# Down-projection weight units taken in pairs, six matmuls in a row to one PSUM bank

## What is computed

```python
def swiglu(h, w_gate, w_up, w_down):
    return (jax.nn.silu(h @ w_gate) * (h @ w_up)) @ w_down

h = rms_norm(x, g_ffn1_pre[l])
x = x + 0.5 * rms_norm(swiglu(h, w_ffn1_gate[l], w_ffn1_up[l], w_ffn1_down[l]), g_ffn1_post[l])
```

## Time and profile before

| | |
|---|---|
| median of 3 runs | 1585.07 us (1584.85 to 1587.95) |
| span of the profiled execution (its whole time isn't recorded apart from the runs above) | 1583.4 us |
| TensorE matmuls busy | 1535.9 us (97%), 6549 |
| VectorE busy | 638.3 us (40%) |
| ScalarE busy | 495.1 us (31%) |
| GpSimd busy | 96.5 us (6%) |
| mean granted TensorE clock | 0.985 of 2.4 GHz |

### The profile page before, as it was taken

One profiled execution on the slowest core, in us unless ns is written; L12 is line 12 of the kernel. 1 busy time (PEld: TensorE's weight loads), 2 busy tenths in 40 slices (PEclk: granted clock), 3 DMA queues, 4 the chain that ended last, 5 costly groups with the idle time before them and its releaser, 6 DMA issues.

```text
span 1583.4 us, 17821 instructions
## 1 busy us (share of the span) xinstructions
PE 1535.9 (97%) x6549; PEld 1213.2 (77%) x6549; DVE 638.3 (40%) x753; ACT 495.1 (31%) x689; POOL 96.5 (6%) x145
## 2 busy tenths in 40 slices
PE   6999999999999979999999999899999999999996
PEld 5888888888888767666657887678888888888884
DVE  4433333333333473435545444463333333333334
ACT  4312212222222343445554232332212222222222
POOL 1000000000000040321220000220000000000001
PEclk9999999999999979999999999899999999999997
DMA  6333333333222212111112334133333333322211
GB/s 208 94 106 93 93 106 93 93 102 107 95 93 93 79 53 82 53 53 54 34 34 68 99 86 133 54 93 93 93 101 93 98 94 93 117 94 93 93 40 54
DMA packets 201007, 138.67 MB, mean 88 GB/s; under 512 B 4448, under 2 KB 188816, under 8 KB 200848
## 3 DMA queue, kind: packets, MB, share of 16 engines
q1 hardware_dynamic: 200160, 135.28, 28.7%
q10 hardware_dynamic: 816, 2.98, 0.5%
HBM read 136.14 MB, written 2.10 MB: 87 GB/s over the span
## 4 chain that ended last, share of the span: by engine, by line
PE 93%; DVE 5%; ACT 1%; DMA 1%; issue 0%; ACTq 0%; POOL 0%; DVEq 0%
PE ps L378 28%; PE ps L379 28%; PE ps L380 28%; PE ps L578 2%; DVE h_lo L916 1%; PE ps L555 1%; DVE ys L911 1%; PE ps L503 1%; PE ps L505 1%; PE ps L504 1%; PE ps L542 1%; PE ps L559 1%; PE ps L546 1%; DVE acc L943 1%; DVE w_lo L888 1%; DMA x_tok<-x 1%
## 5 line engine op out<-in xcount | busy, mean ns | idle before, releaser
L378 PE MATMUL ps<-h_hi,w_hi 128*128 128x512 f32 x1312 | 525.0, 400 | 9.7 <-DVE h_lo L916 7.3
L380 PE MATMUL ps<-h_hi,w_lo 128*128 128x512 f32 x1312 | 512.5, 391 | 0.0
L379 PE MATMUL ps<-h_lo,w_hi 128*128 128x512 f32 x1312 | 512.5, 391 | 0.0
L888 DVE TENSOR_TENSOR w_lo<-w_raw,w_hi 128x1024 fp32r<-128x1024 f32 (+1 forms) x260 | 311.4, 1200 | 172.3 <-ACT w_hi L655 164.1
L378 PEld LDWEIGHTS ps<-h_hi,w_hi 128*128 128x128 f32 x1312 | 247.3, 188 | 79.9 <-issue 24.7
L379 PEld LDWEIGHTS ps<-h_lo,w_hi 128*128 128x128 f32 x1312 | 247.4, 189 | 53.0 <-issue 3.4
L380 PEld LDWEIGHTS ps<-h_hi,w_lo 128*128 128x128 f32 x1312 | 247.2, 188 | 52.5
L655 ACT ACTIVATE w_hi<-w_raw 128x1024 fp32r<-128x1024 f32 (+1 forms) x260 | 257.6, 1019 | 32.5 <-PE ps L380 25.2
L380 PE MATMUL ps<-a_hi,w_lo 128*128 128x512 f32 x512 | 202.2, 395 | 0.0
L378 PE MATMUL ps<-a_hi,w_hi 128*128 128x512 f32 x512 | 202.2, 395 | 0.0
L379 PE MATMUL ps<-a_lo,w_hi 128*128 128x512 f32 x512 | 202.2, 395 | 0.0
(11 more groups left out here) (140 smaller groups left out, 998.4 us busy)
## 6 DMA issues: line engine op xcount, KB each, us to landing
w_raw<-w_ffn_gate SPq DMA_DIRECT2D x64, 512.0 KB, 4.0
w_raw<-w_ffn_up SPq DMA_DIRECT2D x64, 512.0 KB, 4.0
w_raw<-w_ffn_down SPq DMA_DIRECT2D x64, 512.0 KB, 3.3
w_raw<-w_in SPq DMA_DIRECT2D x44, 512.0 KB, 3.8
w_raw<-w_out SPq DMA_DIRECT2D x8, 512.0 KB, 3.7
w_raw<-w_proj_sb SPq DMA_DIRECT2D x8, 256.0 KB, 2.6
w_raw<-w_proj_ret SPq DMA_DIRECT2D x8, 256.0 KB, 2.5
out<-x_tok SPq DMA_DIRECT2D x8, 256.0 KB, 2.7
```

The costliest lines, as they stand in the source:

```text
L378: pe.matmul(ps[:, bank, :], wh, src_hi, start=first, stop=False)
L379: pe.matmul(ps[:, bank, :], wh, src_lo, start=False, stop=False)
L380: return pe.matmul(ps[:, bank, :], wl, src_hi, start=False, stop=last)
L888: dve.tensor_tensor(w_lo[:, slot, 0:cols], w_raw[:, slot, 0:cols], w_hi[:, slot, 0:cols].bitcast(F32), ALU.subtract).then_inc(w_lo_done, 1)
```

## The change

The down-projection on TensorE goes over the weight units in pairs: for each bank it issues the product of the first unit and then that of the second, six matmuls. It waits for both units and both activation blocks ahead of the pair, and adds 2 to `unit_done` after it. The activation parts have four buffers in place of two, and ACT's wait ahead of one is for unit f - 4 in place of f - 2. Weight slots, loads and the order of ACT's and DVE's work stay.

```diff
-        a_hi, e = place("a_hi", [P, 2, T], F32R, at=e)
-        a_lo, e = place("a_lo", [P, 2, T], F32R, at=e)
+        a_hi, e = place("a_hi", [P, SLOTS, T], F32R, at=e)
+        a_lo, e = place("a_lo", [P, SLOTS, T], F32R, at=e)
...
-                def down(f, slot, banks, first=False, last=False):
+                def ready(f):
                     pe.wait_ge(w_lo_done, f + u0 + 2 * NF + 1)
                     pe.wait_ge(a_lo_done, f + NF * fi + 1)
+
+                def down(slot, banks, first=False, last=False):
+
                     for d in banks:
                         if first and d == 0:
                             pe.wait_ge(a_done, NF * (fi + 1))
-                        par = slot % 2
-                        mm = product(d, (slot, d * P), a_hi[:, par, :], a_lo[:, par, :], first, last)
+                        for q in (slot, slot + 1):
+                            mm = product(d, (q, d * P), a_hi[:, q, :], a_lo[:, q, :], first and q == slot,
+                                         last and q == slot + 1)
                         if last and d != banks[-1]:
                             mm.then_inc(y_ready, 1)
-                    mm.then_inc(unit_done, 1)
+                    mm.then_inc(unit_done, 2)
 
                 pe.wait_ge(r_all_ready, 4 * fi + 1)
-                down(0, 0, (4, 5, 6, 7, 0, 1, 2, 3), first=True)
-                with pe.Fori(0, (NF - 3) // SLOTS) as turn:
-                    i = turn * SLOTS + 1
-                    for j in range(SLOTS):
-                        down(i + j, (j + 1) % SLOTS, range(KD))
-                for f in range(NF - 3, NF):
-                    down(f, f % SLOTS, Y_ORDER, last=(f == NF - 1))
+                ready(0)
+                ready(1)
+                down(0, (4, 5, 6, 7, 0, 1, 2, 3), first=True)
+                with pe.Fori(0, NF // SLOTS - 1) as turn:
+                    i = turn * SLOTS + 2
+                    for j in (0, 2):
+                        ready(i + j)
+                        ready(i + j + 1)
+                        down((j + 2) % SLOTS, range(KD))
+                ready(NF - 2)
+                ready(NF - 1)
+                down(2, Y_ORDER, last=True)
...
                 def part(f, par):
                     act_eng.wait_ge(a_done, f + NF * fi + 1)
-                    wait(act_eng, unit_done, f + u0 + 2 * NF - 1)
+                    wait(act_eng, unit_done, f + u0 + 2 * NF - 3)
                     act_eng.activation(a_hi[:, par, :], act[:, f, :], ACT.Copy).then_inc(a_hi_done, 1)
...
-                        part(i * 4 + j + 1, (j + 1) % 2)
+                        part(i * 4 + j + 1, (j + 1) % SLOTS)
```

More of the change, by code:

```diff
@@ L746, in ffn @@
                     if f + 1 < NF:
-                        part(f + 1, (f + 1) % 2)
+                        part(f + 1, (f + 1) % SLOTS)
             def part0(fi):
@@ L1010, in ffn @@
                         split(i + ud + j + AHEAD, (j + AHEAD) % SLOTS)
-                        part(i + j + 1, (j + 1) % 2)
+                        part(i + j + 1, (j + 1) % SLOTS)
                 for f in range(NF - 3, NF):
```

## The result

| | before | after |
|---|---|---|
| median of 4 runs | 1584.96 us | 1750.65 us (1744.56 to 1755.96) |
| span of the profiled execution | 1583.4 us | 1754.2 us |
| mean granted TensorE clock | 0.985 | 0.935 |
| ratio | | 1.1038, interval 1.1011 to 1.1065 |

The changed kernel is slower by 165.7 us. The profiled execution took 1755.96 us, the longest of the four, so its own sum comes to 170.8 us of span.

The account below looks back on a forecast made before the run. The prediction took TensorE, 93% of the chain, to bound the kernel. To 1585.07 us it added 97.2 (pair boundaries), 5.8 (starts) and 44.7 (clock), less 1.4 (ends), +146.3: forecast 1731 us, range 1684 to 1776.

Parts of the forecast that it names:

- The stop at each pair boundary: Down-projections: TensorE waits for the odd activation block, queued behind a weight split; 29 boundaries at 3.35 us, 97.2 us.
- The stop at the start: Start of each down-projection: TensorE also waits for activation block 1, 2.90 us with the restart, twice; 5.8 us.
- The clock: TensorE's granted clock falls to half after pair-boundary stops, one stretch each: 29 x 1.54 = 44.7 us.
- the 2.25 us row: Profile row before the change: after a 2.25 us TensorE gap at 19.42 the clock stood at half; basis for one stretch.
- The end: Last pair of each down-projection: last bank but one ready 0.70 us earlier, so final sums start sooner; -1.4 us.
- Six in a row: Down-projection's new matmul order, six to one bank, costed at nothing; bounds nothing or 10.0 us.
- The loads and SP: Weight loads and the SP queue in the down-projections add nothing.
- the two on the clock: Rivals on the down-projection stops: no clock fall, 1687 us; two half-clock stretches per stop, 1776 us; 12 in 100 each.
- The rival on the faster side: Down-projections: six in a row run at the value projection's pace, gaining 10.0 us; 1579.5 us, 3 in 100.

Follow-up runs that it names:

- e4: Changed kernel plus three float32 matmuls adding zero after each pair but the last, to keep TensorE busy in the stops; 1689.64 us.
- e1: Changed kernel with ACT and DVE taking the part of activation block f ahead of the split of weight unit f+1; 1589.24 us.
- e5: Kernel of e1 with activation block 1 split together with block 0 in the up stage; 1581.59 us.
- e8: As e4, but one float32 matmul by zeros after each pair in place of three, leaving 2.15 us idle; 1704.39 us.
- e2: Changed kernel with the old matmul order, each unit over the banks by itself, three in a row, gating still by pairs; 1752.91 us.
- e6: Kernel before the change with a_hi and a_lo moved 1152 bytes further on in each partition; 1574.77 us.
- e7: Kernel of e5 with a_hi and a_lo moved 1152 bytes, as in e6; 1569.82 us.
- e9: Kernel of e6 with a_hi and a_lo moved by 1024 bytes in place of 1152; 1585.65 us.

## Why the prediction was right, and where it was off

Forecast 1731 us, range 1684 to 1776; measured 1750.65 us, 10.4% slower. The mechanism came as forecast. That the time lies inside the range owes something to its width: it was drawn from no fall of the clock to two stretches per stop, and the measured price lies near the upper of these. By its steps:

- **The stop at each pair boundary** (29, 97.2 us). Right in number, place and chain. Idle 3.01 us where 3.08 was given. The loss of one is read from e4, where the clock stays up. Its first down-projection lasts from 376.15 to 605.34, 229.2 us, against 179.0 us before (373.40 to 552.37); less 1.5 us for one fall of the clock behind the start, 48.7 / 15 = 3.25 us, where 3.35 was forecast. 29 x 3.25 = 94 us. e1 shows the cause: with the activation block ahead of the weight split, the 29 stops are gone.
- **The stop at the start** (5.8 us). Idle 2.72 us where 2.79 was forecast, twice. e5 takes it away. What the forecast left out is the clock there: each of the two brings one stretch at half, 3.1 us together.
- **The clock** (44.7 us). This is the term that was mis-sized: "I take one per stop, being nearest to the 2.25 us row", 29 x 1.54. The changed kernel has 102.4 us at half in the first down-projection and 85.3 us in the second, 55 stretches of 3.41 us for 31 stops, 1.8 each, nearer to the upper bound that I gave (two) than to the value that I took. Measured in the profiled execution, the longest: 170.8 us of span less 94 for the boundaries, less 5.8 for the starts, plus 2.3 gained at the ends, leaves about 73 us. In medians: 61.0 us between the changed kernel and e4, plus 2.6 for e4's filler where there was no stop, plus two falls at the starts that e4 keeps (3.1), 67 us. That is 22 us more than the 44.7, and more than the whole miss of 19 us; the boundaries (3 us less than forecast) and the ends (1 us more gained) take a little back. The choice of the row was the weak step. The gap of 2.25 us was shorter than my stop, and e8 shows how much the length matters. Nor does one row give a mean: the same 3.01 us brought no, one or two stretches.

  The Trainium skill ("TensorE: Matmul & The Clock Gate", HAM oscillation in real kernels) says that bursts parted by waits start again at the low clock each time. Here the clock fell at 30 of the 31 stops of the changed kernel, and in e8, after 2.15 us of idleness, at 12 of 29.
- **The end** (-1.4 us). Before, then after:

```profile
552.37 0.40 PE L380 MATMUL ps<-a_hi,w_lo 128*128 128x512 f32 x1
554.04 1.23 PE L396 MATMUL ps<-cst,acc 128*128 128x1 f32 x8 [1.28 <-DVE acc L943]
```

```profile
643.53 0.40 PE L380 MATMUL ps<-a_hi,w_lo 128*128 128x512 f32 x1
644.05 1.02 PE L396 MATMUL ps<-cst,acc 128*128 128x1 f32 x8
```

Between the last matmul's start and the first sum lay 1.67 us; now it is 0.52 us. That is 1.15 us, twice, -2.3 us. The wait for `acc` is gone altogether, where I had moved it by one addition of 0.70 us only.
- **Six in a row** (nothing). Right: e2 can't be told from the changed kernel, and e6 and e7 have one pace, as the kernel before and e5 have. The Trainium skill's section on psum-queue depth-cycling (same page), by which going round the banks should cost pauses and clock, does not hold here: e6 goes round the banks at 226.7 ns with a granted clock of 1.00.
- **The loads and SP** (nothing). No row of the waits of TensorE, ACT or DVE names a load in the down-projections of the changed kernel.

Of the rivals, the two on the clock enclosed the result: 1687 us (e4, which removes most of the clock's part, gives 1689.64) and 1776 us. The rival on the faster side had its price about right, 10.0 us (e6 gains 10.9), and its cause wrong: it isn't the banks, it is the operand's place.

## What to carry to other kernels

When a producer's release gets coarser (two units at a time), look at every in-order queue for the work that the next step needs and that stands behind the wait for the released slot; swapping the two steps in the queues of ACT and DVE was worth 161 us here. The two more activation buffers did not prevent the stops by themselves; whether the swap would do without them was not tried. Price an idle stop of TensorE together with the clock that it costs, and measure that price with a filler that adds zero. Compare the pace of the same matmul between stages: where it differs with nothing else in the way, try moving the operands.

## What the runs showed of the hardware

A matmul of 128x128 by 128x512 in fp32r runs at 233.3 ns or at 226.7 ns, at the same granted clock, by the place of its right operand. Starting 0 or 1024 bytes past a multiple of 2048 from `h_hi` (and so from the weights) it is fast, at 896 or 1920 slow. By the allocation the address itself is the rounder one in e9, a multiple of 2048, 128 bytes before that of e6, and it is slow; so a round address is not what makes it fast. Two readings are left. It may be the place against the other operands, 0 modulo 1024 being fast. Or it may be the operand's own address modulo 1024: in the fast kernels it is 128, in the slow ones 0. The weights were never moved, so no run parts the two. What in TensorE's reading makes the difference was not tried. The slow pace is not quite one number: e1's first down-projection ran at 232.4 ns, its second and both of e5 at 233.3 ns; why is open.

The best version, e7, takes 1569.82 us: 15.8 us under the kernel before, of which the operands' place makes about 11 and the pairs, fed in time, about 4 to 5 (2.3 of them at the ends, the rest not traced to a place).
